# Second block's mixers: tiles from the seventh on read separately made activations of 256 columns

## What is computed

```python
sh1, sc1, g1, sh2, sc2, g2 = jnp.split(c_act @ w_ada[l] + b_ada[l], 6, axis=-1)
h = rms_norm(x, ln1_g[l]) * (1.0 + sc1) + sh1
z = h @ w_in[l]
u_pool, c_q_raw, c_kv_raw, k_rope_raw, gz_a, gz_b = jnp.split(z, cuts, axis=-1)
y_a = pool_mixer(u_pool, w_pool[l], pool_scale[l]) @ p_pool[l]
y_b = mla(c_q_raw, c_kv_raw, k_rope_raw, ...) @ p_attn[l]
merged = jax.nn.sigmoid(gz_a) * y_a + jax.nn.sigmoid(gz_b) * y_b
x = x + g1 * (merged @ w_out[l])
h2 = rms_norm(x, ln2_g[l]) * (1.0 + sc2) + sh2
x = x + g2 * (jnp.square(jax.nn.relu(h2 @ w_ff1[l])) @ w_ff2[l])
```

## Time and profile before

| | us |
|---|---|
| median of 3 runs | 1828.0 |
| lowest, highest | 1827.34, 1828.42 |
| the profiled execution | 1828.04 |
| its span, first to last instruction | 1826.7 |
| TensorE busy | 1814.2 (99%) |
| VectorE busy | 1362.2 (75%) |
| ScalarE busy | 1046.8 (57%) |
| GpSimd busy | 3.1 (0%) |

### The profile page before, as it was taken

One profiled execution on the slowest core, in us unless ns is written; L12 is line 12 of the kernel. 1 busy time (PEld: TensorE's weight loads), 2 busy tenths in 40 slices (PEclk: granted clock), 3 DMA queues, 4 the chain that ended last, 5 costly groups with the idle time before them and its releaser, 6 DMA issues.

```text
span 1826.7 us, 36565 instructions
## 1 busy us (share of the span) xinstructions
PE 1814.2 (99%) x15035; PEld 1781.2 (98%) x15035; DVE 1362.2 (75%) x2348; ACT 1046.8 (57%) x1735; POOL 3.1 (0%) x9
## 2 busy tenths in 40 slices
PE   9999999999999999999999999999999999999998
PEld 9999999999999999999899999999999999999998
DVE  7887786677886788678667887787887559788754
ACT  6454675665444545467656554686665458666533
POOL 0000000000000000000000000000000000000000
PEclk9999999999999999999999999999999999999999
DMA  8887443467785778644357887455566655556663
GB/s 294 308 279 239 128 142 102 136 195 251 264 318 160 226 262 296 211 137 139 109 162 228 280 294 268 136 180 159 178 184 184 191 177 172 154 171 190 183 192 106
DMA packets 92566, 364.59 MB, mean 200 GB/s; under 512 B 11148, under 2 KB 12076, under 8 KB 86256
## 3 DMA queue, kind: packets, MB, share of 16 engines
q1 hardware_dynamic: 91968, 361.46, 62.3%
q10 hardware_dynamic: 432, 0.79, 0.1%
HBM read 361.15 MB, written 1.05 MB: 198 GB/s over the span
## 4 chain that ended last, share of the span: by engine, by line
PE 90%; DVE 6%; ACT 2%; issue 1%; DMA 1%; SPq 0%; DVEq 0%; ACTq 0%
PE bank L567 27%; PE bank L569 27%; PE bank L568 27%; PE bank L627 2%; DVE w_lo L1754 2%; PE bank L623 1%; PE bank L624 1%; ACT w_hi L1197 1%; PE bank L849 1%; PE bank L864 1%; PE bank L894 0%; DVE s_pool L2264 0%; DMA ada_raw<-in_ada_w 0%; PE bank L801 0%; PE bank L1025 0%
## 5 line engine op out<-in xcount | busy, mean ns | idle before, releaser
L567 PE MATMUL bank<-xn_hi,w_hi 128*128 128x272 f32 (+2 forms) x2640 | 758.5, 287 | 0.4 <-DVE w_lo L1754 0.2
L569 PE MATMUL bank<-xn_lo,w_hi 128*128 128x272 f32 (+2 forms) x2640 | 749.1, 284 | 0.0
L568 PE MATMUL bank<-xn_hi,w_lo 128*128 128x272 f32 (+2 forms) x2640 | 748.9, 284 | 0.0
L567 PEld LDWEIGHTS bank<-xn_hi,w_hi 128*128 128x128 f32 x2640 | 498.2, 189 | 8.1 <-issue 6.2
L568 PEld LDWEIGHTS bank<-xn_hi,w_lo 128*128 128x128 f32 x2640 | 498.2, 189 | 0.7
L569 PEld LDWEIGHTS bank<-xn_lo,w_hi 128*128 128x128 f32 x2640 | 498.2, 189 | 0.0
L1197 ACT ACTIVATE w_hi<-raw_a 128x1024 fp32r<-128x1024 f32 (+2 forms) x278 | 302.2, 1087 | 276.1 <-PE bank L569 258.5
L1197 ACT ACTIVATE w_hi<-raw_b 128x1024 fp32r<-128x1024 f32 (+3 forms) x280 | 305.3, 1090 | 260.0 <-PE bank L569 252.2
L1754 DVE TENSOR_TENSOR w_lo<-raw_b,w_hi 128x1024 fp32r<-128x1024 f32 (+3 forms) x280 | 353.8, 1263 | 130.0 <-ACT w_hi L1197 127.7
L1754 DVE TENSOR_TENSOR w_lo<-raw_a,w_hi 128x1024 fp32r<-128x1024 f32 (+1 forms) x276 | 349.2, 1266 | 126.0 <-ACT w_hi L1197 124.7
L567 PE MATMUL bank<-h_hi,w_hi 128*128 128x272 f32 (+1 forms) x704 | 200.7, 285 | 0.2 <-DVE full L1953 0.2
(11 more groups left out here) (357 smaller groups left out, 2629.5 us busy)
## 6 DMA issues: line engine op xcount, KB each, us to landing
raw_b<-in_weights SPq DMA_DIRECT2D x244, 512.0 KB, 3.6
raw_a<-in_weights SPq DMA_DIRECT2D x240, 512.0 KB, 3.6
ada_raw<-in_ada_w SPq DMA_DIRECT2D x48, 1024.0 KB, 4.9
raw_a<-in_weights SPq DMA_DIRECT2D x32, 704.0 KB, 5.2
raw_b<-in_weights SPq DMA_DIRECT2D x32, 704.0 KB, 5.3
raw_b<-in_weights SPq DMA_DIRECT2D x6, 256.0 KB, 4.7
c_rows<-in_c_rows SPq DMA_DIRECT2D x3, 512.0 KB, 4.6
raw_a<-in_weights SPq DMA_DIRECT2D x4, 384.0 KB, 3.3
```

What stands on the lines that cost most here:

```text
L567: pe.matmul(o, wh, xh, start=start, stop=False)
L568: pe.matmul(o, wl, xh, start=False, stop=False)
L569: return pe.matmul(o, wh, xl, start=False, stop=stop)
```

## The change

From step 6 on (`MIX_SCALED`), the tiles of z's projection no longer read `xn` with its 258 columns, but new buffers `z_hi` and `z_lo` of 256 columns that hold the normalised, scaled and shifted activations. They are made meanwhile: VectorE multiplies x by gain and rstd (`z_scale`, into one of two buffers, the two halves of `s_pool`), ScalarE adds the shift and rounds to the high part (`z_high`), VectorE subtracts to get the low part (`z_low`). Three of the eight k-tiles are made before step 0, five in steps 0 to 4. TensorE waits before step 6 for the last low part. For tiles from step 6 on VectorE's `scaled_tile` falls away; ScalarE waits for the unit itself and reads the bank, with a copy for u_pool and with tanh for the gates; it then frees the bank. To make room, `scores`, `pt2` and `a2` are placed in `xn`'s buffer. `z_shift` and `z_scaled` also take a stage "ff", which the change does not use.

```diff
--- before.py
+++ after.py
@@ -228,7 +228,9 @@
             return tuple(sb(name + part, [P, tiles, width], F32R, 256, 224 if width == N else past) for part, past in (("_hi", 0), ("_lo", 128)))
 
         self.x = sb("x", [P, KD, T])
+        xn_at = place
         self.xn_hi, self.xn_lo = streamed("xn", KD)
+        xn_end = place
         self.sumsq, self.sq, self.sq2 = (sb(n, [P, T]) for n in ("sumsq", "sq", "sq2"))
 
         self.sq_pair = nc.alloc_sbuf_tensor_at("sq_pair", [P, 2, T], F32, offset=place - 4 * 2 * T)
@@ -316,10 +318,14 @@
         self.k_rot = sb("k_rot", [96, N])
         self.q_all, self.k_all = sb("q_all", [96, MH, N]), sb("k_all", [96, MH, N])
         self.v_tok, self.r_tmp = sb("v_tok", [P, 2, 512]), sb("r_tmp", [P, N])
-        self.scores, self.pt2, self.stat2 = sb("scores", [P, 2, 3 * P]), sb("pt2", [P, 4, 3 * P]), sb("stat2", [P, 32])
+        self.stat2 = sb("stat2", [P, 32])
+        self.z_hi, self.z_lo = streamed("z", KD, N)
+        assert place <= end - 8 * N - 64
+
+        place = xn_at
+        self.scores, self.pt2 = sb("scores", [P, 2, 3 * P]), sb("pt2", [P, 4, 3 * P])
         self.a2_hi, self.a2_lo = streamed("a2", 4, N)
-
-        assert place <= end - 8 * N - 64
+        assert place <= xn_end
         place = latent
         self.y2_hi, self.y2_lo = streamed("y2", KD, N)
 
@@ -348,6 +354,9 @@
 def gate_up_bank(i, b):
 
     return 4 + b if i % 2 and b < 2 else b
+
+
+MIX_SCALED = 6
 
 
 def is_moved(at):
@@ -430,6 +439,17 @@
 def both_ways(c, j):
 
     return (c.full, c.gate)[j][:, 0, :]
+
+
+def z_shift(c, stage, kk):
+
+    col = (24 if stage[0] == "ff" else 0) + kk
+    return c.mod_all[:, stage[1], col:col + 1]
+
+
+def z_scaled(c, stage, kk):
+
+    return ((c.sq, c.sq2)[kk % 2] if stage[0] == "ff" else c.s_pool[:, kk % 2, :])[:, 0:N]
 
 
 def finish(chains, place):
@@ -1116,9 +1136,13 @@
             if is_moved(at):
                 if at == 5:
                     rope_keys(u, b, l)
+                elif at >= MIX_SCALED:
+                    if at == MIX_SCALED:
+                        pe.wait_ge(*k.at("x_lo", ("z", *stage, KD - 1)))
+                    tile(u, b, TN, c.z_hi, c.z_lo)
                 elif at > 3:
                     tile(u, b, TX, *streams(c, stage))
-                free[b] = [("tile_v", ("n2", l, at))]
+                free[b] = [("tile_v", ("n2", l, at)) if at < MIX_SCALED else ("tile_a", ("pool", l, at - 6) if at < 10 else ("gate", l, gate_of(at)))]
             elif at in (12, 13):
                 queries(u, at - 12, l)
                 if at == 13:
@@ -1243,6 +1267,11 @@
             two_norms(stage)
         else:
             root_of_mean(7, LIVE[stage[1]] if stage[0] == "ffn" and stage[2] else TA if stage[0] == "ffn" else TB, stage)
+
+    def z_high(stage, kk):
+
+        act.wait_ge(*k.at("scaled", ("z", *stage, kk)))
+        act.activation(c.z_hi[:, kk, :], z_scaled(c, stage, kk), ACT.Identity, bias=z_shift(c, stage, kk)).then_inc(*k.up("x_hi", ("z", *stage, kk)))
 
     def two_norms(stage):
 
@@ -1621,17 +1650,24 @@
         squares = [c.sq2[:, 0:N], c.gate[:, 0, 0:N], c.gate[:, 1, 0:N], c.sq[:, 0:N], c.full[:, 0, 0:N]]
         chains = [(3, 12, latent(l, "cq", 3, QL, c.cq, c.cq_hi)), (5, 13, latent(l, "ckv", 2, KVL, c.ckv, c.ckv_hi)),
                   (6, 12, k_rope(l)), (9, 14, pooled(l)), (17, 35, attention2(l))]
+        for kk in range(3):
+            z_high(stage, kk)
         u = u0
         for at in range(47):
             finish(chains, at)
             if at < 39:
                 split_hi(u + 4)
+            if at < 5:
+                z_high(stage, at + 3)
             if at == 9:
                 load_table(EXP_TANH_SET)
             elif at == 41:
                 load_table(LN_EXP_SET)
             if is_moved(at):
-                act.wait_ge(*k.at("tile_v", ("n2", l, at)))
+                if at < MIX_SCALED:
+                    act.wait_ge(*k.at("tile_v", ("n2", l, at)))
+                else:
+                    act.wait_ge(k.sem["unit_done"], u + 1)
                 if at < 5:
                     name, kk, t = ("cq", at, c.cq_x) if at < 3 else ("ckv", at - 3, c.ckv_x)
                     s = t[:, kk, N:N + 1]
@@ -1641,12 +1677,11 @@
                     act.activation(c.k_rot[RP, :], c.full[0:32, 1, 0:N], ACT.Identity, bias=c.full[0:32, 1, N:N + 1]).then_inc(*k.up("tile_a"))
                     act.activation(c.r_tmp[RP, :], c.full[32:64, 1, 0:N], ACT.Identity, bias=c.full[32:64, 1, N:N + 1]).then_inc(*k.up("tile_a", ("krope", l)))
                 elif at < 10:
-                    t = c.u_pool[:, at - 6, META:T]
-                    act.activation(t, t, ACT.Identity, bias=c.u_pool[:, at - 6, T:T + 1]).then_inc(*k.up("tile_a", ("pool", l, at - 6)))
+                    act.activation(c.u_pool[:, at - 6, META:T], bank[moved_bank(at)][:, 0:N], ACT.Copy).then_inc(*k.up("tile_a", ("pool", l, at - 6)))
                 else:
 
                     j = gate_of(at)
-                    act.activation(c.gates2[:, j, :], c.gates2[:, j, :], ACT.Tanh, bias=c.gates2_x[:, j, N + 1:N + 2], scale=0.5).then_inc(*k.up("tile_a", ("gate", l, j)))
+                    act.activation(c.gates2[:, j, :], bank[moved_bank(at)][:, 0:N], ACT.Tanh, scale=0.5).then_inc(*k.up("tile_a", ("gate", l, j)))
                 if 22 < at < 27:
                     g = at - 23
                     act.wait_ge(*k.at("tile_a", ("pw", l, g)))
@@ -1827,6 +1862,23 @@
             two_norms(stage)
         dve.wait_ge(*k.at("rstd", stage))
 
+    def z_scale(stage, kk):
+
+        dve.scalar_tensor_tensor(out=z_scaled(c, stage, kk), in0=c.x[:, kk, TB], scalar=c.gain[:, stage[1], int(stage[0] == "ff"), kk:kk + 1], in1=c.rstd[:, TB],
+                                 op0=ALU.mult, op1=ALU.mult).then_inc(*k.up("scaled", ("z", *stage, kk)))
+
+    def z_low(stage, kk):
+
+        if kk == 0:
+            z_scale(stage, 0)
+        if kk + 1 < KD:
+            if kk:
+                dve.wait_ge(*k.at("x_lo", ("z", *stage, kk - 1)))
+            z_scale(stage, kk + 1)
+        dve.wait_ge(*k.at("x_hi", ("z", *stage, kk)))
+        dve.scalar_tensor_tensor(out=c.z_lo[:, kk, :], in0=z_scaled(c, stage, kk), scalar=z_shift(c, stage, kk), in1=c.z_hi[:, kk, :].bitcast(F32),
+                                 op0=ALU.add, op1=ALU.subtract).then_inc(*k.up("x_lo", ("z", *stage, kk)))
+
     def scaled_tile(u, dst, b, key, rows=P):
 
         dve.wait_ge(k.sem["unit_done"], u + 1)
@@ -2306,6 +2358,8 @@
         chains = [(5, 13, latent(l, "ckv", 2, c.sq[:, 0:N], [c.full[:, 0, 0:N]], c.ckv, c.ckv_hi, c.ckv_lo, V_KVG)),
                   (3, 12, latent(l, "cq", 3, c.sq2[:, 0:N], [c.gate[:, 0, 0:N], c.gate[:, 1, 0:N]], c.cq, c.cq_hi, c.cq_lo, V_QG)),
                   (6, 13, k_rope(l)), (8, 15, pooled(l)), (13, 15, q_rope(l)), (17, 35, attention2(l))]
+        for kk in range(3):
+            z_low(stage, kk)
         u = u0
         for at in range(47):
             finish(chains, at)
@@ -2313,10 +2367,8 @@
                 scaled_tile(u, c.cq_x[:, at, :] if at < 3 else c.ckv_x[:, at - 3, :], moved_bank(at), ("n2", l, at))
             elif at == 5:
                 scaled_tile(u, c.full[0:64, 1, TX], 5, ("n2", l, at), rows=64)
-            elif at < 10:
-                scaled_tile(u, c.u_pool[:, at - 6, META:T + 2], moved_bank(at), ("n2", l, at))
-            elif is_moved(at):
-                scaled_tile(u, c.gates2_x[:, gate_of(at), :], moved_bank(at), ("n2", l, at))
+            if at < 5:
+                z_low(stage, at + 3)
             if l == 0 and 26 < at < 31:
                 in_place(TB, c.vg[:, G_FN:G_FN + 8], c.rstd2[:, :], "fn", range(2 * at - 54, 2 * at - 52))
                 if at == 30:
```

## The result

The changed kernel takes 1830.57 us (median of 20 runs, 1829.44 to 1832.26), the kernel before 1827.68 us in the same session (20 runs, 1826.97 to 1829.12). The ratio is 1.0016, 95% interval 1.0010 to 1.0022: slower by 0.16%, 2.9 us. The forecast was 1830.1 us, within 0.2% of no change. The time came out 0.5 us from it, but the sum behind it misses two things that pull opposite ways: a loss at a low clock (2.5 us in the profiled execution, about 1.4 in the medians) and about 1 us of saving. The experiments take them apart.

The account below looks back on a forecast made before the run. TensorE, 99% busy at full clock, was taken to bound the kernel; -3.1 + 4.1 + 1.1 = +2.1 us on 1828.0 gave 1830.1 us. Forecast range 1829.0 to 1831.5 (chance 0.65); 8 in 10: 1827.0 to 1832.7.

Parts of the forecast that it names:

- the sum behind it: Whole kernel: narrower tiles -3.1 us, layer 0's stalls +4.1, layer 1's +1.1, together +2.1 us.
- The schedule of layer 0: Layer 0's mixer, first tiles: making z delays VectorE, so TensorE waits 0.5 and 3.2 us; loss 4.1 us with restarts.
- Layer 1: Layer 1's mixer: VectorE's idle time hides 2.2 us; TensorE waits 0.9 us for the cq sum, loss 1.1 us.
- The saving: TensorE's matmuls from tile 6 on, both layers: 3.1 us less, bounds 1.9 to 3.4 us.
- Part 1: Tiles from 6 on: 960 matmuls go from 258 to 256 columns, 3.2 ns each, -3.1 us.
- part 2: Tiles from 6 on: VectorE loses 20 scalings per layer, ScalarE reads banks directly; TensorE never waited for either, worth nothing.
- columns' share: Rival for the narrower tiles: two columns save only 0.8 ns per matmul; with the stalls 1832.4 us; chance 0.05.
- The clock: Rival: the clock falls in layer 0's 3.2 us wait for the cq sum, adding 2.0 us: 1832.1; chance 0.14.
- a granted clock under 1.00 in the stretch after the break: Sign in the changed profile that the forecast is wrong: TensorE's clock below its top level after its new wait.
- z's wait before tile 6: Before tile 6, layer 0: TensorE's wait for z's last low part costs nothing once the other stalls are paid.
- The rival that z's work hides: First tiles of the mixers: both stalls vanish, leaving -3.1 us, 1824.9; with halfway case 1827, chance together 0.14.

Follow-up runs that it names:

- experiment 1: Changed kernel's layout and narrow tiles, but z never made (GpSimd writes zeros into its buffers once per layer): 1824.29 us beside 1827.89 for the kernel before.
- experiment 2: Changed kernel with seven unused fp32 matmuls filling TensorE's wait for the cq sum in layer 0: 1829.14 us beside 1827.89 for the kernel before.
- experiments 3: Changed kernel with VectorE adding the cq squares before z's scaling 7 and low part 6: 1829.07 us beside 1827.89 for the kernel before.
- experiment 7: Changed kernel with TensorE summing the cq squares after tile 6 instead of after tile 4: 1836.07 us beside 1827.50 for the kernel before.
- experiment 5: Changed kernel with z's scaling on GpSimd, parts made in steps 1 to 8, z used from step 10: 1842.84 us beside 1827.63 for the kernel before.
- experiments 2 and 4: 2 has its own line; 4: the change in layer 1 alone, layer 0 as in the kernel before: 1827.02 us beside 1827.89 for the kernel before.

## Why the prediction was right, and where it was not

*The schedule of layer 0* held nearly to the figure. Forecast: tile 0 scaled 3.2 us late, a stall of 0.5 for unit 4, then 3.2 for the cq sum. In the trace: 3.3 (1171.19 after the end of rstd at 1167.86), 0.58 and 3.06. The writing-out from rows, with start-to-start times in place of durations, was enough. *Layer 1* was forecast with a wait of 0.9, and had about 1.0. This part was right by its mechanism, not by luck.

*The saving* was mis-sized: 3.1 forecast, 4.2 found by experiment 1 (in the mixers' windows; 3.6 by the medians). Part 1, the narrower tiles, held: 3.0 to 3.3 ns per matmul in the changed kernel, 3.2 forecast. The step that failed is part 2, "TensorE never waited for either: worth nothing", argued from a list of waits that hides breaks as short as a matmul's overlap. Some 1.2 us of such breaks fell away, 0.6 us per layer, at the first unit of the values and at the tile after them. A columns' share of 0.8 us in all is ruled out. The Trainium skill (TensorE: Matmul & The Clock Gate, section "Back-to-back issue gap") has, for an isolated matmul, a start-to-start time that grows by 1/2.4 ns per column; the section itself says that a stream of weight loads and matmuls, as here, keeps another pace. The runs do not agree with it: 3.0 to 3.3 ns for two columns, not 0.8.

*The clock* was a rival, with a chance of 0.14 and a price of 2.0 us. In the profiled execution it came true, at 2.5 us (experiment 2). In the forecast's own sum it was missing. The place and the cause, the 3.1 us break in layer 0, were as the rival said, and "a granted clock under 1.00 in the stretch after the break" stood among the prediction's signs of being wrong. Whether 0.14 was too low one case cannot tell, but in the profiles here all five breaks of 2.3 us and more (one in the changed kernel, one each in experiments 3 and 7, two in experiment 5) had it. The Trainium skill (TensorE: Matmul & The Clock Gate, section "What's actually happening") says that the default is throttled and activity lifts it; the rows now agree, with 0.50 after breaks of 3.1 and 2.3 us and 1.00 after the breaks of about 1 us in experiments 2 and 4.

*The sum*, in the profile: 6.7 us lost in layer 0 (0.8 for unit 4, 3.2 for the sum, 2.7 at the low clock by the spacing of the starts) and 1.3 in layer 1, less 4.2: +3.8, which is the change of the two mixers' windows (4.46 - 0.68). The forecast had +2.1. With a fall of about 1.4 us in place of 2.7 it would be +2.5; the median went up by 2.9. So the result lies near the forecast partly by luck: a rival's loss and an unforeseen gain cancel.

*z's wait before tile 6*, called free once the others are paid, was absent in the trace, as forecast. But the prediction added that without the others it would have been within 0.3 us of binding. Experiment 7 shows more: without the sum's wait ahead of it, it is 3.0 us, because z is itself late. By the prediction's own times too, z is ready at 1182.3 and unit 6 would start at 1178.9.

*The rival that z's work hides* fell, though VectorE's load in the stretch in which z is made is no higher than its mean. The windows of the kernel before, from rstd to unit 6, in layer 0 and layer 1 (busy columns: TensorE, its weight loads, VectorE, ScalarE, GpSimd):

```profile
1168.60:1179.00 10.40, 10.40 (x88) 10.21 (x87) 7.83 (x12) 8.41 (x16) 0.00 (x0) 1.00 0.62 197
1493.80:1507.00 13.20, 13.20 (x111) 13.03 (x110) 7.71 (x13) 8.72 (x16) 0.00 (x0) 1.00 0.62 189
```

VectorE is busy for 75% and 58%, which leaves 2.6 and 5.5 us free. z needs 6.4. As an estimate, 3.8 and 0.9 us are too much; TensorE's waits in these steps are 3.6 (0.58 + 3.06) and 1.0 us. A share of 25% is little room when the stretch is only 10 us long.

## What to carry to other kernels

Extra work for an engine that is not the bound is priced by its free microseconds in the stretch in which it must be done, and not by its mean load: here 6.4 us of VectorE's work met 2.6 free us in one layer and cost TensorE 3.6 us of waits, and 5.5 free us in the next, which has one norm less ahead of it, and cost 1.0. Whoever must put it there puts it behind the small steps for which the bounding engine waits. A break of TensorE of 2 to 3 us has a second price in the clock: 2.5 us in one profiled execution, about 1.4 in the medians. Short breaks are counted by the distances between matmul starts, not by the list of waits.

## What was unexpected in the hardware

- A break of 2.3 us was followed by about 3 us of work at the low clock (0.50), one of 3.0 us (experiment 7) by about the same, one of 3.1 us by 5.6 us; breaks of 1.0 us were not. What sets the length of the stay is open.
- Two columns more in the moving operand cost 3.0 to 3.3 ns per matmul, 258 against 256 columns; the formula quoted above would make 0.8.
- GpSimd's elementwise work on SBUF stretched VectorE's: the same 128 x 1024 subtraction took 1.36 to 1.75 us instead of 1.23.
- A matmul's shown duration hides breaks: 0.32 us of delay appeared as 0.15, and 0.2 us did not appear at all.
